# The last of 32 gathered experts taken out of its group: down piece in column halves, outputs added by 32-row products

## The reference, cut to what matters

```python
# h: 256 x 1024 after norm and modulation; every token takes 2 of 32 experts (of one group of 8)
def expert_block(xblk, e):
    hid = silu(xblk @ w_gate[e]) * (xblk @ w_up[e])      # 1024 -> 512
    return hid @ w_down[e]                               # 512 -> 1024
y = sum over the token's two experts of weight * expert_block(token, e)
x = x + g2 * y
return x * rsqrt(mean(x * x) + 1e-6) * final_g
```

## Time and profile before

| | us |
|---|---|
| median of 3 runs (lowest to highest) | 917.6 (916.29 to 918.64) |
| span of the profiled execution | 916.1 |
| PE busy in it | 780.7 (85%) |
| PE weight loads | 469.3 (51%) |
| DVE busy | 373.1 (41%) |
| ACT busy | 170.1 (19%) |

### The profile page before, as it was taken

One profiled execution on the slowest core, in us unless ns is written; L12 is line 12 of the kernel. 1 busy time (PEld: TensorE's weight loads), 2 busy tenths in 40 slices (PEclk: granted clock), 3 DMA queues, 4 the chain that ended last, 5 costly groups with the idle time before them and its releaser, 6 DMA issues.

```text
span 916.1 us, 13144 instructions
## 1 busy us (share of the span) xinstructions
PE 780.7 (85%) x5441; PEld 469.3 (51%) x5441; DVE 373.1 (41%) x881; ACT 170.1 (19%) x473; POOL 39.6 (4%) x36
## 2 busy tenths in 40 slices
PE   7999899999998999998999997758667777677675
PEld 4544664456577544466477573535435445345332
DVE  2478678567855776536342311111111110121113
ACT  3223631213356210023120100000000000001001
POOL 1110000014300000000000000000000000000000
PEclk9999999999999999999999997999988998799879
DMA  9983507665004559961979999999999999999994
GB/s 346 395 306 129 184 1 279 227 231 183 1 1 146 211 171 382 397 254 68 391 275 398 430 426 427 429 428 429 430 426 429 427 430 428 429 429 426 429 424 166
DMA packets 54123, 284.39 MB, mean 310 GB/s; under 512 B 2752, under 2 KB 7232, under 8 KB 41408
## 3 DMA queue, kind: packets, MB, share of 16 engines
q1 hardware_dynamic: 54080, 283.81, 77.1%
HBM read 282.75 MB, written 1.05 MB: 310 GB/s over the span
## 4 chain that ended last, share of the span: by engine, by line
PE 55%; DMA 34%; DVE 5%; issue 2%; ACT 2%; POOL 1%; SPq 1%; DVEq 0%; POOLq 0%
DMA ring<-in_up_w 30%; PE banks L1906 15%; PE banks L1772 13%; PE banks L2270 8%; PE banks L1856 3%; DMA ring<-in_down_w 2%; PE banks L2318 2%; PE banks L1804 2%; PE banks L2255 2%; PE banks L1841 1%; DMA ring<-in_ada_w 1%; POOL rs L559 1%; DVE soft L1052 1%; PE banks L1884 1%; ACT probs L633 1%
## 5 line engine op out<-in xcount | busy, mean ns | idle before, releaser
L2270 PE MATMUL banks<-ring,QT 128*32 128x256 f32 x1696 | 144.4, 450 | 58.0 <-DMA ring<-in_up_w 58.0
L1906 PE MATMUL banks<-ring,hT 128*128 128x512 f32 (+4 forms) x384 | 156.7, 562 | 2.2 <-DMA ring<-in_ab_w 2.0
L1772 PE MATMUL banks<-ring,hT 128*128 128x512 f32 x320 | 141.6, 600 | 2.7 <-issue 1.5
L2270 PEld LDWEIGHTS banks<-ring,QT 128*32 128x32 f32 x1696 | 72.7, 125 | 108.3 <-DMA ring<-in_up_w 43.6
L1906 PEld LDWEIGHTS banks<-ring,hT 128*128 128x128 f32 x384 | 72.0, 192 | 74.8 <-issue 67.9
L1668 DVE TENSOR_TENSOR QT<-banks,MOD 32x256 f32<-32x256 f32 x128 | 53.8, 420 | 137.9 <-PE banks L2318 136.7
L1772 PEld LDWEIGHTS banks<-ring,hT 128*128 128x128 f32 x320 | 60.7, 192 | 80.2 <-issue 75.0
L1659 DVE TENSOR_TENSOR QT<-QT,banks 64x256 f32<-64x256 f32 x32 | 13.5, 423 | 190.9 <-ACT QT L901 190.9
L2318 PE MATMUL banks<-ring,QT 128*32 128x256 f32 x992 | 66.7, 412 | 14.8 <-ACT QT L908 12.4
L559 POOL TENSOR_TENSOR rs<-st,mhalf 128x1 f32<-128x1 f32 (+7 forms) x27 | 32.4, 1203 | 870.6 <-DVE st L1705 448.9
L901 ACT ACTIVATE QT<-banks 64x256 f32<-64x256 f32 x32 | 12.0, 375 | 293.1 <-PE banks L2270 293.1
(11 more groups left out here) (353 smaller groups left out, 712.9 us busy)
## 6 DMA issues: line engine op xcount, KB each, us to landing
ring<-in_up_w SPq DMA_DIRECT2D x30, 2048.0 KB, 23.8
ring<-in_down_w SPq DMA_DIRECT2D x30, 2048.0 KB, 21.8
ring<-in_gate_w SPq DMA_DIRECT2D x23, 2048.0 KB, 20.5
ring<-in_ada_w SPq DMA_DIRECT2D x12, 2048.0 KB, 15.4
probs<-in_gate_w SPq DMA_DIRECT2D x8, 2048.0 KB, 29.3
ring<-in_ab_w SPq DMA_DIRECT2D x4, 2048.0 KB, 19.6
ring<-in_cd_w SPq DMA_DIRECT2D x4, 2048.0 KB, 13.6
ring<-in_in_w SPq DMA_DIRECT2D x4, 2048.0 KB, 14.5
```

The lines of the kernel that those rows point to most:

```text
L1772: ins = pe.matmul(bank[j % 4][:, 0:n], hT[:, k, t * P:(t + 1) * P], w[:, k, :], start=(k == 0), stop=(k == KD - 1))
L1906: ins = pe.matmul(bank[b][:, 0:n], hT[:, k, t * P:(t + 1) * P], w[:, k, :], start=(k == 0), stop=(k == KD - 1))
L2270: return pe.matmul(bank[1][CAP * j:CAP * j + CAP, 0:256], XG[:, k, CAP * s:CAP * s + CAP], wk[:, :, 2 * (j % 2):2 * (j % 2) + 2], start=(k ...
```

## The change

The last expert (31) is taken out of the sum of group 7. `add_outputs(7)` now adds three experts (96 rows) and stands ahead of `gate_up(31)`; `gate_up(31)` itself moves from behind `turn_hidden(30)` to behind that sum. In the transfers down 30 moves ahead of gate 31 and up 31, to its usual place. Down 31 still comes in two halves, now halves of the columns: `down_last(half)` makes four strips of 128 columns in `bank[half]`, one DVE instruction scales all four strips at once (`outputs_last`), and `add_last(half)` adds them with eight products of 32 rows, 128 columns, in two turns of four; the four of a turn take the four different row strips and the four different banks. For that the 32 columns of expert 31 in the selection matrix are repeated four times and turned (`spread_last`, `turn_spread`), and g2 is laid out by strips (`gate_strips`). The sum's banks hold the columns in another order (`by_bank`, `sum_bank`, `sum_half`). ACT takes the squares once all 16 `sums` are counted, in two instructions over 1024 columns in place of four over 512, and the final instructions of DVE stand in another order.

```diff
--- before.py
+++ after.py
@@ -222,10 +222,26 @@
         ones = qt_flat[:, 2688:2816]
         YE = qt_flat[:, 2816:3840]
+        def by_bank(a):
+            return a.rearrange("p (h b n) -> p b h n", h=2, b=2)
+        def sum_bank(t, b):
+            return bank[4 + 2 * t + b][:, :].rearrange("p (h n) -> p h n", h=2)
+        def sum_half(t, h):
+            return banks[:, 4 + 2 * t:6 + 2 * t, 256 * h:256 * h + 256]
+        def in_halves(a):
+            return a.rearrange("p (b n) -> p b n", b=2)
         def spare(a):
             return Y[:, 0, 2048 + a:2304 + a].rearrange("p (t n) -> p t n", t=NT)
         SEL, SW, SWT = spare(0), spare(256), spare(512)
+        gate_strips, last_out = [MOD[:, 1, 256 * i:256 * i + 256].rearrange("p (h n) -> p h n", h=2) for i in range(2)]
+        last_spread, last_spreadT = [MOD[:, 2, 256 * i:256 * i + 256].rearrange("p (t n) -> p t n", t=NT) for i in range(2)]
         chunks = []
@@ -519,19 +535,15 @@
                 load_gathered(4, 5, 1)
                 load_gathered(0, 6, 2)
                 load_gathered(5, 5, 3)
-                for e in range(6, NE - 2):
-                    for j in range(1 if e == 6 else 0, 3):
+                for e in range(6, NE):
+                    for j in range(1 if e == 6 else 0, 2 if e == NE - 1 else 3):
                         once_in_four = e % 2 == 0 and j == 0
                         load_gathered(3 * (e % 2) + j, e, e - 4 if once_in_four else e - 2)
-                for e in (NE - 2, NE - 1):
-                    for j in range(2):
-                        load_gathered(3 * (e % 2) + j, e, e - 4 if e % 2 == 0 and j == 0 else e - 2)
-                load_gathered(2, NE - 2, NE - 4)
                 sp.wait_ge(*upto("g_down", NE - 2))
                 down = srcs[2](NE - 1)
                 for half in range(2):
-                    sp.dma_start(ring[eslot(5)][:, 2048 * half:2048 * half + 2048].rearrange("p (k n) -> p k n", k=2),
-                                 down[:, 2 * half:2 * half + 2, :]).then_inc(sem(f"last_down{half}"), 16)
+                    sp.dma_start(ring[eslot(5)][:, 2048 * half:2048 * half + 2048].rearrange("p (k n) -> p k n", k=FC),
+                                 down[:, :, 512 * half:512 * half + 512]).then_inc(sem(f"last_down{half}"), 16)
             with sp.Else():
                 load_pairs(dense_free)
             for t in range(NT):
@@ -917,9 +929,9 @@
                     if e % 4 == 3 and e // 4 + 1 < QUADS:
                         for half in range(2):
                             take_tokens(e // 4 + 1, half)
-                for b in range(4):
-                    act.wait_ge(*upto("sums", b + 1))
-                    sumsq(bank[4 + b][:, :], st[:, b:b + 1], "sum_ss", Y[:, b // 2, D + 512 * (b % 2):D + 512 * (b % 2) + 512])
+                act.wait_ge(*upto("sums", 16))
+                for t in range(NT):
+                    sumsq(banks[:, 4 + 2 * t:6 + 2 * t, :], st[:, t:t + 1], "sum_ss", in_halves(Y[:, t, D:2 * D]))
             with act.Else():
                 silu_gates(0, True)
                 with act.Fori(1, NE) as e:
@@ -1674,7 +1686,28 @@
                 v.wait_ge(*upto("g_swt", q + 1))
                 if q > 0:
                     v.wait_ge(*upto("g_add", q))
+                if last_quad(q):
+                    v.tensor_copy(last_spreadT, bank[0][:, 256:512].rearrange("p (t n) -> p t n", t=NT))
                 v.tensor_copy(SWT, bank[0][:, 0:256].rearrange("p (t n) -> p t n", t=NT)).then_inc(sem("g_swc"), 1)
+            def spread_last():
+                v.wait_ge(*upto("g_sw", QUADS))
+                v.tensor_copy(by_expert(last_spread), SW[:, :, 3 * CAP:4 * CAP].unsqueeze(2).to_broadcast([P, NT, 4, CAP]))\
+                 .then_inc(sem("g_swr"), 1)
+                for n in range(4):
+                    strip = slice(CAP * n, CAP * n + CAP)
+                    ins = v.tensor_copy(gate_strips[strip, :, :],
+                                        MOD[strip, 5, :].rearrange("p (h s n) -> p s h n", h=2, s=4)[:, n, :, :])
+                ins.then_inc(sem("g_strips"), 1)
+            def outputs_last(half):
+                v.wait_ge(*upto("g_last", half + 1))
+                if half == 0:
+                    v.wait_ge(*upto("g_strips", 1))
+                v.tensor_tensor(last_out[:, half, :], bank[half][:, 0:P], gate_strips[:, half, :], ALU.mult)\
+                 .then_inc(sem("g_yl"), 1)
             link(v.tensor_reduce(st[:, 0:1], bank[2][:, 2 * NE:3 * NE], AX.X, ALU.max))
@@ -1689,25 +1722,36 @@
             with v.If(crowded == 0):
                 for e in range(NE):
                     q = e // 4
-                    if e < NE - 1:
-                        hidden(e)
-                    if e == NE - 2:
-                        hidden(NE - 1)
+                    hidden(e)
                     if e % 4 == 0:
                         turned(q)
                         if q + 1 < QUADS:
                             select(q + 1)
                             spread(q + 1)
-                    outputs(e)
-                for t in range(NT):
-                    o = slice(2 * t, 2 * t + 1)
-                    v.wait_ge(*upto("sum_ss", 2 * t + 2))
-                    go(v.tensor_scalar(st2[:, t:t + 1], st[:, o], st[:, 2 * t + 1:2 * t + 2], D * EPS, ALU.add, ALU.add), "ms")
-                    rooted()
-                    for c in range(2):
-                        cols = slice(512 * c, 512 * c + 512)
-                        v.scalar_tensor_tensor(out=X[:, t, cols], in0=bank[4 + 2 * t + c][:, :], scalar=rs[:, t:t + 1],
-                                               in1=MOD[:, 0, cols], op0=ALU.mult, op1=ALU.mult).then_inc(sem("out"), 1)
+                        if q + 1 == QUADS - 1:
+                            spread_last()
+                    if e < NE - 1:
+                        outputs(e)
+                for half in range(2):
+                    outputs_last(half)
+                def final_mean(t):
+                    v.wait_ge(*upto("sum_ss", t + 1))
+                    means(1, 1.0, a=t, eps=D * EPS)
+                def final_rows(t, c):
+                    cols = slice(512 * c, 512 * c + 512)
+                    v.scalar_tensor_tensor(out=in_halves(X[:, t, cols]), in0=sum_half(t, c), scalar=rs[:, t:t + 1],
+                                           in1=in_halves(MOD[:, 0, cols]), op0=ALU.mult, op1=ALU.mult).then_inc(sem("out"), 1)
+                final_mean(0)
+                rooted()
+                final_rows(0, 0)
+                final_mean(1)
+                final_rows(0, 1)
+                rooted()
+                final_rows(1, 0)
+                final_rows(1, 1)
             with v.Else():
                 dense_experts()
                 for t in range(NT):
@@ -2184,7 +2228,7 @@
             def keep_residual(t, c):
                 pe.wait_ge(*upto("wout_x", 3 + t))
-                return pe.matmul(bank[4 + 2 * t + c][:, :], ident, X[:, t, 512 * c:512 * c + 512], start=True, stop=False)
+                return pe.matmul(sum_bank(t, c), ident, by_bank(X[:, t, :])[:, c, :, :], start=True, stop=False)
             def route(t):
                 rows_copied("mx", t)
@@ -2304,39 +2348,67 @@
             def down(q, s):
                 e, last = expert_of(q, s)
-                if not last:
-                    gathered_landed(pe, q, s, 2)
+                gathered_landed(pe, q, s, 2)
                 pe.wait_ge(*upto("g_hc", e + 1))
                 if last_quad(q):
                     pe.wait_ge(*upto("g_ye", e))
                 wd = gathered_weight(q, s, 2)
                 for c in range(FC):
-                    if last and c % 2 == 0:
-                        pe.wait_ge(*upto(f"last_down{c // 2}", 16))
                     a = 64 * (c % 2) + CAP * (c // 2)
                     for n in range(4):
                         ins = pe.matmul(bank[2][CAP * n:CAP * n + CAP, 0:256], HG[:, a:a + CAP],
                                         wd(c)[:, 256 * n:256 * n + 256], start=(c == 0), stop=(c == FC - 1))
                 ins.then_inc(sem("g_down"), 1)
+            def down_last(half):
+                if half == 0:
+                    pe.wait_ge(*upto("g_hc", NE))
+                pe.wait_ge(*upto(f"last_down{half}", 16))
+                for c in range(FC):
+                    a = 64 * (c % 2) + CAP * (c // 2)
+                    at = 2048 * half + 512 * c
+                    for n in range(4):
+                        ins = pe.matmul(bank[half][CAP * n:CAP * n + CAP, 0:P], HG[:, a:a + CAP],
+                                        ring[eslot(5)][:, at + P * n:at + P * n + P], start=(c == 0), stop=(c == FC - 1))
+                ins.then_inc(sem("g_last"), 1)
+            def add_last(half):
+                pe.wait_ge(*upto("g_yl", half + 1))
+                for turn in range(2):
+                    if half + turn > 0:
+                        pe.wait_ge(*upto("sums", 8 * half + 4 * turn))
```

(41 more changed lines are left out.)

## The result

The changed kernel takes 922.6 us in the median of nine runs (919.1 to 926.0), the kernel before 917.6 in nine beside them (915.8 to 920.0). The ratio over the runs is 1.0047, with a 95% interval of 1.0028 to 1.0065: slower by 0.5%, as forecast (922.0). The profiled execution has a span of 922.8 at a mean clock of 0.944; its own time is 924.6, which lies 2.0 over the median.

A forecast was written before the change was run, and what follows sets the result against it. Transfers set the end until 903.0, computation after; with PE 4.8 us behind the last landing, terms gave a span of 920.6, +4.5 on 916.1. Adding 1.5 and rounding for 96 rows gave 922.0, range 918.8 to 924.8.

The forecast's parts named there:

- rival B: PE idle 893.6 to 895.5: clock falls, sum and part of gate_up(31) run at half speed; 924.4, chance 0.15.
- The transfers: Loads of the last experts: gate 31 lands at 893.2, up 31 at 898.1, last landing stays at 903.0.
- three signs of being wrong: Wrong if gate_up(31) begins before 897, the last landing moves, or the end needs under 6.5 us from the last add.
- PE up to `gate_up(31)`: PE's queue: down(30) 1.93, DVE scaling 1.72, group sum 3.7 to 899.2, then gate_up(31) 6.58 to 905.8.
- The narrow forms: Last expert's end: column-half down products 2.0 us, four turns of 32-row adds 2.8, squares to last scaled rows 5.1.
- Rival C: In the 32-row adds: narrow adds do not overlap, a turn costs 1.04, +1.6; 923.6, chance 0.08.
- Edits at nothing: Extra transposes and copies, spread_last, the moved SP issue and reordered columns: hidden under waits, no cost.
- the tail: From last scaled rows to the end of the span, issue and landing of the last output: 2.9 us, as before.
- Rival A: In gate_up(30): clock up earlier, 3.85 us instead of 6.2, everything behind 2.3 earlier; 919.7, chance 0.12.
- Rival D: At the last expert: landing of up 31, not the group sum, holds gate_up(31); end 917.6, chance 0.05.
- that balance: Last expert's products 8.0 us later, 4.8 behind the landing; shorter scaling and adds return about two, uncovered squares take that again.

The follow-up runs named there:

- e5_after_again: The changed kernel itself, unchanged, timed and profiled once more; ratio to the kernel before 1.0040 [1.0022, 1.0058].
- e2_four_strips: The changed kernel with gate_up(31) making its four strips side by side instead of two and two; ratio to the kernel before 1.0037 [1.0023, 1.0052].
- e10_mended: The changed kernel with four strips in gate_up(31), the sum's fourth product behind it, idle products ahead of the sum, one raise per turn; ratio to before 1.0004.
- e12_row_pieces: The changed kernel with down 31 loaded in row halves (8 KB pieces), both awaited before the column products; ratio to the kernel before 1.0054 [1.0036, 1.0072].
- e11_end_alone: The kernel before, order and halves kept, with only two 1024-column squares behind all four sums and DVE's last steps reordered; ratio to before 1.0019.
- e4_order_alone: The kernel before with only the new order of loads and queues, expert 31 added by 32-row, 512-column products; ratio to before 1.0077 [1.0056, 1.0099].
- e1_order_back: The changed kernel with the old order of loads and of DVE's and PE's steps, new end kept; ratio to the kernel before 1.0046 [1.0029, 1.0062].

## Why the prediction was right

Its chain of PE, step by step, behind the zero at `gate_up(30)`; the forecast's zero was 883.49, and `e5_after_again` is the execution without B.

| step | forecast | after | e5 |
|---|---|---|---|
| start of `gate_up(30)` | 883.49 | 882.18 | 882.24 |
| sum begins | 12.0 | 12.4 | 12.3 |
| `gate_up(31)` begins | 15.7 | 17.7 | 15.9 |
| last down products begin | 24.3 | 26.3 | 24.5 |
| squares begin | 29.1 | 30.9 | 29.1 |
| last rows end | 34.2 | 35.7 | 33.9 |
| end of the span | 37.1 | 40.6 | 38.0 |

*The transfers.* Gate 31 was forecast to land at 893.2 and up 31 at 898.1, behind a zero at 883.49, so 9.7 and 14.6 later; they came 9.7 and 14.6 behind theirs, and the last half 19.7 behind, where it was 19.5 before: the last landing has not moved. None of the three signs of being wrong came: `gate_up(31)` began at 899.9, and the end took 9.9 us from the last add.

*PE up to `gate_up(31)`.* Right: `gate_up(31)` begins behind the sum, whose own wait DVE ends, and not behind a landing. The terms 1.93, 1.72, 3.67 and 6.58 are those of the rows. That PE comes last, by 4.8, is borne out by `e2_four_strips` and `e10_mended`: PE reached the last down piece 3.0 and 3.8 earlier than in `e5_after_again`, and the last rows ended 3.0 and 4.1 earlier.

*The narrow forms.* Forecast 2.0 for both halves, measured 1.95; 2.8 for four turns, measured 910.41 to 913.03, 2.6. Squares to last rows: 5.1 forecast, 4.85 measured. Rival C is out.

*Edits at nothing.* The 2 KB pieces under the cover of a late PE: `e12_row_pieces` bears that out.

*Mis-sized, the tail.* "The span ended 2.9 later" was taken over from before; it measured 4.9 and 4.05. It's the one term of the sum that is off by over a us (the fallen clock stood as a rival). In the changed kernel's profile 1.1 of it is the last output held back behind a slow issue. The rest, landings of 2.6 to 4.0 us in place of 2.0 to 2.6, has no known cause. It is not the one queue (3.96 with two), not the 2 KB pieces (4.7 without), not the close order of the four outputs by itself (2.8 in `e11_end_alone`). It was 3.4 in `e4_order_alone` and 3.8 in `e10_mended`.

*Mis-sized, rival B.* Held for a case of 0.15 and 924.4. It was in the profiled execution of after, at +1.7 rather than the 2.4 assumed for half of 4.8 us, and absent in `e5_after_again`. It is a matter of the execution, and of no single order: two of the four falls came in the old order of the queue. The tail and the fall together, with the zero 1.3 earlier and small terms of -0.2, make 920.6 - 1.3 + 1.7 + 2.0 - 0.2 = 922.8, the measured span.

*What was luck.* The path is right; that the medians came as near as 5.0 and 4.5 against the 4.4 of the forecast is in part luck. Counted from the common zero the two profiles end 8.0 and 5.4 later than before, of which 2.0 and 1.2 are the tail that the sum didn't have. How often the clock falls in the runs that make up the medians isn't known, those of before included, since only one run of each is profiled.

*Rival A* (the clock up earlier in `gate_up(30)`) did not come in the profiled execution, 6.58 us for that product; a part of it is seen in others, 5.14 at the least, and that is a matter of the execution too.

*Rival D* (landings still set the last expert, level with before) fell with the start of `gate_up(31)`. It took `e10_mended`, with `gate_up(31)` begun 14.8 behind the zero, 0.2 behind the landing of up 31, to bring about the level time that D described.

*Two costs, not one.* `e4_order_alone` is at +6.7 and `e11_end_alone` at +2.4, and the whole change at 4.5 to 5.0, less than their sum of 9.1. `e4_order_alone` pays for the order with the old end, `e11_end_alone` for the uncovered squares without the narrow scaling and adds, so the two need not add up. The forecast had that balance: 8.0 us of which 4.8 are behind the landing, about two given back, the squares taking that again. What the narrow end does where PE is early wasn't run; an estimate is 9.2 us from the start of the narrow products to the last rows (29.8 - 20.6 in `e10_mended`) against 10.2 from the last landing before (29.75 - 19.54), about 1 us better, less what the longer tail takes. That squares of one half can't run beside the adds of the other, since each bank holds columns of both halves, is argued from the code and wasn't tried.

## What to carry to other kernels

Work that is moved ahead of a transfer's wait is free only if its engine isn't the one that comes last; find, for the engine's own queue, how many us it is ahead of the last landing (here 2.3), and move no more than that in front of what needs it. An end made to shorten the way behind the last transfer won back only 1.7 of the 6.7 us that the new order cost: look for the engine's lateness first and split the moved block so that its rest fills the waits behind it, as the fourth product did. Compare profiles from a common event, and profile an unchanged kernel twice before an effect of the clock is put down to an edit: the filled gap looked like a cure until the unfilled one did the same.

## What the runs showed of the hardware

- The granted clock fell to 0.50 around the sum in 4 of 14 profiles. It fell while PE was at work again behind an idle time: 0.2 us into the sum behind 1.93 in after and `e12_row_pieces`, about 1.3 us into it behind 1.33 in `e1_order_back`, and about 1.4 us into `down(31)` behind 1.28 in `e11_end_alone`. It stayed at full with the same idle time of 1.93 in `e2_four_strips` and `e5_after_again`, and of 1.94 in before. The sum took 1.7 us more each time.
- `gate_up(30)`, the same instructions behind the same landing, took from 5.14 to 6.58 us up to ACT's first step on it, with the granted clock at 0.50 from its start in all 14 profiles and up again sooner or later within it.
- Outputs of 256 KB landed in 2.0 to 2.1 us in `e11_end_alone` and 2.6 to 4.0 in the changed kernel, and one issue took up to 1.72 us where others take 0.33. With issues of 0.57 at most on two queues the landings were still 2.6 to 3.5. I have no cause for it.
- Eight passes of 512 columns took 4.26 us over 32 rows, 3.67 over 96.
